# State-space mixer: C stationary in 32-column blocks, heads of a pair alternating, decay per sequence made once

## What is computed

```python
acum = jnp.cumsum(dtc * A_gr, axis=1)
decay = jnp.exp(jnp.where(causal, acum[:, :, None] - acum[:, None, :], -jnp.inf))
cb = jnp.einsum('btgn,bsgn->btsg', Cc, Bc)
wts = cb[..., None] * decay * dtc[:, None]
y = jnp.einsum('btsgr,bsgrp->btgrp', wts, xc)
y = y + jnp.einsum('btgn,bgrpn->btgrp', Cc, hs) * jnp.exp(acum)[..., None]
hs = exp(acum[:, -1]) * hs + jnp.einsum('bsgr,bsgrp,bsgn->bgrpn', to_end, xc, Bc)
```

## Time and profile before

| | us |
|---|---|
| median of 3 runs | 3431.39 |
| lowest, highest | 3429.54, 3434.74 |
| span of the profiled execution | 3425.9 |
| state-space stage in it | about 1534 to 2484 |

### The profile page before, as it was taken

The page is one execution under the profiler, slowest core; times in us unless marked ns, Lnnn a source line. Parts: engine busy times, 40 slices in busy tenths (PEclk is TensorE's granted clock), DMA queues, the critical chain, the costliest instruction groups (busy, mean ns, idle before and its releaser), DMA issues.

```text
span 3425.9 us, 64127 instructions
## 1 busy us (share of the span) xinstructions
PE 3279.2 (96%) x23449; PEld 3192.2 (93%) x23449; DVE 2114.1 (62%) x3198; ACT 1350.2 (39%) x1691; POOL 887.6 (26%) x1123
## 2 busy tenths in 40 slices
PE   7999999999999999989999999999989999999997
PEld 6999999999999999988888988988889999999997
DVE  4554556676546675567676676676666674467644
ACT  4332324444334444443343333343344543344432
POOL 2101013222102232225442343243332230023221
PEclk9999999999999999999999999998899999999999
DMA  5343435444454444544444444444434444544444
GB/s 201 137 164 135 174 114 181 147 169 162 145 173 160 171 159 147 172 166 166 157 157 158 157 163 157 168 158 170 169 119 164 166 156 151 172 168 161 161 148 145
DMA packets 91384, 545.56 MB, mean 159 GB/s; under 512 B 11688, under 2 KB 12528, under 8 KB 43904
## 3 DMA queue, kind: packets, MB, share of 16 engines
q1 hardware_dynamic: 71872, 466.98, 38.6%
q0 software_dynamic: 19392, 76.98, 6.2%
HBM read 510.92 MB, written 32.99 MB: 159 GB/s over the span
## 4 chain that ended last, share of the span: by engine, by line
PE 80%; DVE 8%; issue 6%; ACT 4%; POOL 2%; DMA 0%; DVEq 0%; POOLq 0%; ACTq 0%; SPq 0%
PE ps L388 25%; PE ps L389 24%; PE ps L390 24%; PE ps L395 7%; ACT w_hi L660 2%; DVE w_lo L983 2%; DVE b_u L1312 1%; DVE b_u L1314 1%; DVE b_u L1310 0%; DVE work L1397 0%; DVE sumsq L1392 0%; POOL sumsq L1470 0%; POOL b_xw L1614 0%; DVE b_s L1386 0%; ACT b_out_hi L937 0%
## 5 line engine op out<-in xcount | busy, mean ns | idle before, releaser
L388 PE MATMUL ps<-hn_hi,w_hi 128*128 128x288 f32 x4896 | 1481.3, 303 | 36.9 <-DVE w_lo L983 16.8
L389 PE MATMUL ps<-hn_lo,w_hi 128*128 128x288 f32 x4896 | 1461.8, 299 | 0.0
L390 PE MATMUL ps<-hn_hi,w_lo 128*128 128x288 f32 x4896 | 1456.0, 297 | 0.0
L983 DVE TENSOR_TENSOR w_lo<-w_raw,w_hi 128x2048 fp32r<-128x2048 f32 (+1 forms) x482 | 1045.0, 2168 | 593.3 <-ACT w_hi L660 593.0
L660 ACT ACTIVATE w_hi<-w_raw 128x2048 fp32r<-128x2048 f32 (+1 forms) x482 | 857.7, 1780 | 1145.2 <-PE ps L390 1140.5
L388 PEld LDWEIGHTS ps<-hn_hi,w_hi 128*128 128x128 f32 x4896 | 936.9, 191 | 45.8 <-issue 22.1
L389 PEld LDWEIGHTS ps<-hn_lo,w_hi 128*128 128x128 f32 x4896 | 938.0, 192 | 1.2
L390 PEld LDWEIGHTS ps<-hn_hi,w_lo 128*128 128x128 f32 x4896 | 938.6, 192 | 0.0
L1546 POOL COPY f_new<-f_pad 128x2 f32 x176 | 242.6, 1379 | 1080.9 <-ACT f_u L831 1080.9
L388 PE MATMUL ps<-act_hi,w_hi 128*128 128x288 f32 x1408 | 416.2, 296 | 13.8 <-DVE act_lo L1242 13.8
L389 PE MATMUL ps<-act_lo,w_hi 128*128 128x288 f32 x1408 | 418.0, 297 | 0.0
(11 more groups left out here) (261 smaller groups left out, 3462.2 us busy)
## 6 DMA issues: line engine op xcount, KB each, us to landing
w_raw<-wf_up_in SPq DMA_DIRECT2D x176, 1024.0 KB, 4.8
w_raw<-wf_down_in SPq DMA_DIRECT2D x128, 704.0 KB, 4.0
w_raw<-wb_in_in SPq DMA_DIRECT2D x80, 1024.0 KB, 4.8
w_raw<-wa_in_in SPq DMA_DIRECT2D x48, 1024.0 KB, 4.8
w_raw<-wb_out_in SPq DMA_DIRECT2D x32, 1024.0 KB, 4.8
w_raw<-wa_out_in SPq DMA_DIRECT2D x16, 1024.0 KB, 4.8
b_sT<-b_sT_in POOLq DMA_DIRECT2D x32, 512.0 KB, 4.9
b_s<-b_s_in POOLq DMA_DIRECT2D x32, 512.0 KB, 4.4
```

Of the source, the lines that this page charges most:

```text
L388: nc.tensor.matmul(out, w_hi[:, s, col], hi[:, t, :], start=first and k == 0, stop=False)
L389: nc.tensor.matmul(out, w_hi[:, s, col], lo[:, t, :], start=False, stop=False)
L390: m = nc.tensor.matmul(out, w_lo[:, s, col], hi[:, t, :], start=False, stop=end)
L983: TT(w_lo[:, s, 0:cols], w_raw[:, s, 0:cols], w_hi[:, s, 0:cols].bitcast(F32), ALU.subtract).then_inc(w_low, 1)
```

## The change

- The product of C with the carried state moves from "mix" to "sel". For each sequence b a block of 32 columns (`b_cm_of[b]`, C of its four tokens, zero elsewhere) is stationary, and the 128 columns of the sequence's state `b_sT[:, b, :]` move. Sequences share four column blocks of the array (output partitions 32g to 32g+31, g = b % 4), two accumulated on each. `b_sT_in` is awaited here. ScalarE scales the result by the decay per token and head (`b_eas`) into `b_ys`, ahead of its exponential, and one matmul with `fold` (four stacked 32x32 identities) adds it to the output's PSUM inside the mix.
- In the mix the two heads of a pair alternate block by block, and the sample block takes 128 rows of `b_xdt` and `b_dec`, whose rows past 32 are zero, for 32.
- The decay of the sample tokens and of the states is made once in `gate_columns_b`, for all heads (`b_eas`, `b_fade`), not per pair from `b_rsum` and `b_ea`; GpSimd's state decay reads `b_fade`.
- VectorE's output is one instruction where it was three.
- GpSimd adds the squares of pairs 1 and 2 to those of pair 0, and the mean takes two matmuls for four.

The load `b_sT` keeps its place in GpSimd's order. The diff, cut to the lines that change and one before them:

```diff
@@ -223,10 +224,11 @@
             b_u = sb("b_u", [P, BP], F32, st)
-            b_yi = sb("b_yi", [P, TS], F32, st)
-            b_rows = sb("b_rows", [64, 3, T], F32, st)
+            b_rows = sb("b_rows", [P, 3, T], F32, st)
             b_nac2 = sb("b_nac2", [P, T], F32R, st)
-            b_rsum = sb("b_rsum", [64, TS + 1], F32, st)
+            b_amp = sb("b_amp", [64, 1], F32, st)
+            b_fade = sb("b_fade", [P, 32, NB], F32, st)
+            b_eas = sb("b_eas", [P, 64], F32, st)
@@ -239,11 +241,14 @@
             b_xw = sb("b_xw", [P, 3, P], F32, st)
-            b_ea = sb("b_ea", [P, TS], F32, st)
         b_tmp = b_xdt[0:64, 0:2, 0:T]
+        b_ea4 = b_xdt[0:64, 0, 0:P].rearrange("p (j t) -> p j t", j=4)
+        b_spread = b_xdt[0:64, 1, 0:64 * NB]
+        b_cm = b_rows[:, 1, :].rearrange("p (b x) -> p b x", x=TS + SL)
+        b_cm_of = [b_rows[:, 1, TS * b:TS * (b + 1)] for b in range(NB)]
+        b_ys = b_rows[:, 2, 0:P]
@@ -553,14 +561,18 @@
                         m = nc.tensor.transpose(ps[0:w, M1 if n < 2 else M2, 192 * (n % 2) + 64 * b:192 * (n % 2) + 64 * b + 64],
-                                                b_rows[:, row, b * P:b * P + w], ident[0:64, 0:64])
-                m.then_inc(gb_turned, 1)
+                                                b_rows[0:64, row, b * P:b * P + w], ident[0:64, 0:64])
+                pe.wait_ge(gb_faded, 1)
+                nc.tensor.transpose(ps[:, M2, 192:256], b_xdt[0:64, 0, 0:P], ident[0:64, 0:64])
+                pe.wait_ge(gb_spread, 1)
+                mm(ps[:, M3, :], mean_mat[0:64, :], b_spread).then_inc(gb_turned, 1)
                     wait(pe, b_gvar, u)
+                    wait(pe, b_ysr, u.times(4))
@@ -581,25 +593,28 @@
                     mm(ps[:, M0, 0:T], b_sel[:, 0, :], b_nac2[:])
-                    mm(ps[:, M1, 0:T], b_sel[:, 1, :], b_nac2[:])
-                    one_head = b_sel[0:64, :, :].bitcast(F32)
-                    mm(ps[0:64, M1, T:T + TS], one_head[:, 0, 0:64], b_rsum[:, 0:TS])
-                    mm(ps[64:P, M1, T:T + TS], one_head[:, 1, 0:64], b_rsum[:, 0:TS]).then_inc(b_rowsr, 1)
+                    mm(ps[:, M1, 0:T], b_sel[:, 1, :], b_nac2[:]).then_inc(b_rowsr, 1)
+                    wait(pe, b_cmr, u.plus(1))
+                    wait(pe, b_spr, u.times(4).plus(k))
+                    wait(pe, b_sT_in, u.times(4).plus(k + 1).times(16))
+                    for b in range(NB):
+                        g = b % 4
+                        m = mm(ps[TS * g:TS * (g + 1), M3, P:2 * P], b_cm_of[b], b_sT[:, b, :], b < 4, b >= 4)
+                    m.then_inc(b_yraw, 1)
                     k = (j - 2) // 2
-                    ch = slice(k * P, (k + 1) * P)
                     wait(pe, b_yg, u.times(4).plus(k))
-                    wait(pe, b_sT_in, u.times(4).plus(k + 1).times(16))
-                    for b in range(NB):
-                        mm(ps[:, M2, T + SL * b:T + SL * (b + 1)], b_sT[:, b, :], cT[:, TP + SL * b:TP + SL * (b + 1)])
-                    for e in range(2):
-                        rows, hc = slice(64 * e, 64 * (e + 1)), slice(k * P + 64 * e, k * P + 64 * (e + 1))
+                    wait(pe, b_ysr, u.times(4).plus(k + 1))
+                    halves = [(slice(64 * e, 64 * (e + 1)), slice(k * P + 64 * e, k * P + 64 * (e + 1))) for e in range(2)]
+                    for e, (rows, hc) in enumerate(halves):
                         mm(ps[rows, M2, 0:TP], b_xdt[:, 0, hc], b_dec[:, e, 0:TP], True, False)
+                    for e, (rows, hc) in enumerate(halves):
                         mm(ps[rows, M2, P:TP], b_xdt[:, 1, hc], b_dec[:, e, TP:TP + P], False, False)
-                        m = mm(ps[rows, M2, TP:T], b_xdt[0:TS, 2, hc], b_dec[0:TS, e, TP + P:SC], False, True)
-                    m.then_inc(b_yst, 1)
+                    for e, (rows, hc) in enumerate(halves):
+                        mm(ps[rows, M2, TP:T], b_xdt[:, 2, hc], b_dec[:, e, TP + P:SC], False, False)
+                    mm(ps[:, M2, TP:T], b_ys, fold[:], False, True).then_inc(b_yst, 1)
@@ -608,11 +623,11 @@
                 if j == 9:
+                    wait(pe, b_gsum, u.plus(1).times(2))
+                    wait(pe, b_yg, u.plus(1).times(4))
+                    mm(ps[:, M2, 0:T], mean_mat[:], b_io[:, p, 2, :], True, False)
                     wait(pe, b_gsq, u.plus(1).times(4))
-                    wait(pe, b_yg, u.plus(1).times(4))
-                    for k in range(4):
-                        m = mm(ps[:, M2, 0:T], mean_mat[:], b_io[:, p, 2 + k, :], k == 0, k == 3)
-                    m.then_inc(b_gms, 1)
+                    mm(ps[:, M2, 0:T], mean_mat[:], b_io[:, p, 5, :], False, True).then_inc(b_gms, 1)
@@ -854,18 +869,19 @@
                     wait(act, proj_taken, EA_BGATE + 1)
-                    own.link(A(b_rows[:, 1, :], b_rows[:, 1, :], ACT.Identity, bias=b_small[:, 0:1]))
-                    A(b_rsum[:, TS:TS + 1], b_small[:, 1:2], ACT.Exp)
-                    own.link(A(b_tmp[:, 0, :], b_rows[:, 1, :], ACT.Abs))
-                    A(b_rows[:, 2, :], b_tmp[:, 0, :], ACT.Exp, scale=-1.0).then_inc(gb_exp, 1)
+                    own.link(A(b_rows[0:64, 1, :], b_rows[0:64, 1, :], ACT.Identity, bias=b_small[:, 0:1]))
+                    A(b_amp[:], b_small[:, 1:2], ACT.Exp)
+                    own.link(A(b_tmp[:, 0, :], b_rows[0:64, 1, :], ACT.Abs))
+                    A(b_rows[0:64, 2, :], b_tmp[:, 0, :], ACT.Exp, scale=-1.0).then_inc(gb_exp, 1)
                     act.wait_ge(gb_logs, 1)
-                    A(b_nac2[0:64, :], b_rows[:, 0, :], ACT.Copy).then_inc(gb_high, 1)
-                    A(b_rows[:, 2, :], b_rows[:, 2, :], ACT.Exp, scale=-1.0)
-                    A(b_rsum[:, 0:TS], b_rows[:, 0, TP:T], ACT.Exp, scale=-1.0).then_inc(gb_rows, 1)
+                    A(b_nac2[0:64, :], b_rows[0:64, 0, :], ACT.Copy).then_inc(gb_high, 1)
+                    A(b_rows[0:64, 2, :], b_rows[0:64, 2, :], ACT.Exp, scale=-1.0).then_inc(gb_rows, 1)
+                    A(b_ea4, b_rows[0:64, 0, TP:T].unsqueeze(1).to_broadcast([64, 4, TS]), ACT.Exp,
+                      scale=-1.0).then_inc(gb_faded, 1)
@@ -874,7 +890,12 @@
                         w = P if b < 2 else TS
-                        m = A(col[0:w, :, b, :], src[0:w, :, b, :], ACT.Copy)
+                        A(col[0:w, :, b, :], src[0:w, :, b, :], ACT.Copy)
+                A(b_eas[:], ps[:, M2, 192:256], ACT.Copy)
+                for e in range(2):
+                    rows = slice(64 * e, 64 * (e + 1))
+                    m = A(b_fade[rows, :, :], ps[rows, M3, :].rearrange("p (m e b) -> p e m b", e=2, b=NB)[:, e, :, :],
+                          ACT.Copy, scale=float(D_MODEL))
@@ -915,6 +936,14 @@
                     k = (j - 2) // 2
+                    n = u.times(4).plus(k)
+                    wait(act, b_yraw, n.plus(1))
+                    wait(act, b_yst, n.times(2))
+                    for e in range(2):
+                        head = n.times(2).plus(e).value
+                        col = slice(head, head + 1) if isinstance(head, int) else bass.ds(head, 1)
+                        m = A(b_ys[:, 64 * e:64 * (e + 1)], ps[:, M3, P + 64 * e:P + 64 * (e + 1)], ACT.Copy, scale=b_eas[:, col])
+                    m.then_inc(b_ysr, 1)
@@ -1042,6 +1071,9 @@
             TS_(b_normw[:], b_normw[:], 0.5, None, ALU.mult)
+            own.link(TT(fold[:], ident[:, 0:TS], ident[:, TS:2 * TS], ALU.add))
+            own.link(TT(fold[:], fold[:], ident[:, 2 * TS:3 * TS], ALU.add))
+            TT(fold[:], fold[:], ident[:, 3 * TS:P], ALU.add)
@@ -1258,10 +1290,11 @@
             V.memset(b_dec[:], 0.0)
+            V.memset(b_xdt[:, 2, :], 0.0)
             norm(2)
-            TT(b_rows[:, 1, :], ps[0:64, (N_BIN - 1) % 4, 0:T], rstd[0:64, :], ALU.mult).then_inc(proj_taken, 1)
-            brow = lambda n: b_rows[:, n, :] if n < 3 else b_tmp[:, n - 3, :]
+            TT(b_rows[0:64, 1, :], ps[0:64, (N_BIN - 1) % 4, 0:T], rstd[0:64, :], ALU.mult).then_inc(proj_taken, 1)
+            brow = lambda n: b_rows[0:64, n, :] if n < 3 else b_tmp[:, n - 3, :]
@@ -1279,13 +1312,16 @@
-                    own.link(TS_(brow(4), brow(1), b_rsum[:, TS:TS + 1], None, ALU.mult))
+                    own.link(TS_(brow(4), brow(1), b_amp[:], None, ALU.mult))
                     dve.wait_ge(gb_high, 1)
-                    TT(b_nac2[64:P, :], b_rows[:, 0, :], b_nac2[0:64, :].bitcast(F32), ALU.subtract).then_inc(gb_low, 1)
+                    TT(b_nac2[64:P, :], b_rows[0:64, 0, :], b_nac2[0:64, :].bitcast(F32), ALU.subtract).then_inc(gb_low, 1)
+                    dve.wait_ge(gb_faded, 1)
+                    TT(b_spread.rearrange("p (h b) -> p h b", b=NB), head_ident[0:64, :].unsqueeze(2).to_broadcast([64, 64, NB]),
+                       b_ea4[:, 0, SL - 1:TS:SL].unsqueeze(1).to_broadcast([64, 64, NB]), ALU.mult).then_inc(gb_spread, 1)
                 if j == 7:
```

(20 more changed lines are left out.)

7 lines of the change are left out of this document (4 added, 3 removed).

## The result

The changed kernel takes 3474.38 us (median of 4 runs, 3469.54 to 3486.12), the kernel before 3431.89 beside it: ratio 1.0133, 95% interval 1.0113 to 1.0152. It is slower by 42.5 us, as forecast (3472). The profiled execution has a span of 3471.7 for 3425.9.

A forecast was written before the change was run, and what follows sets the result against it. TensorE's line was taken as bound, neck and neck with VectorE's order; six steady groups 34, first group 3.5, last 0, gate columns 3.4, together 41 us on span 3425.9, plus 5.5 to the median: 3472 us, range 3425 to 3520.

The forecast's parts named there:

- The wait: Sel of pairs 1 to 3: TensorE idles 3 to 5 us for the b_sT load, some 24 times, 100 us in all.
- The steady group: Six of the eight mixed groups, walked pair by pair: each turn, 105.61 us before, grows by 5.7 us.
- The clock's p: Projection behind each b_sT wait: what the lowered clock adds, 2.2 to 3.8 us, taken as 2.5.
- the columns: New 32-column matmuls in sel: four column blocks at once, 0.75 us per pair.
- The rival of no overlap: Column blocks and heads run serially: sel 2.0 us, b_dec 1.65, 4.6 more per group, 3507 us; chance 0.12.
- The groups: State-space stage: six steady groups add 34 us, the first group 3.5, the last about 0.
- The gate columns: Once, before TensorE restarts at the gate columns: spread product, 512-column matmul, copies and three more add 3.4 us.
- The squares: Two of four mean matmuls go, 1.0 us per group; GpSimd's additions, 1.5 us each, cost nothing or lie under the exponential.
- The other side: Rival: the load is in time, each group gains 4 us, 32 in all, less 3.4, giving 3403 us; chance 0.12.

The follow-up runs named there:

- the early load: Changed kernel with GpSimd issuing the b_sT load of the next pair one step earlier, behind the b_s load: 3389.9 us, ratio 0.988 to the kernel before.
- The filled wait: Changed kernel with 24 projection-size matmuls that nobody reads ahead of TensorE's b_sT wait in pairs 1 to 3: 3457.42 us, ratio 1.0083.

## Why the prediction came out as it did

**The wait** was the prediction's core, and it stands: 24 waits for `b_sT` of 4.7 us in the mean, 113.5 in all (predicted 3 to 5 each, 100 in all), and the early load removes both them and the loss. The load lands 6.0 to 7.3 us behind the additions, 6.6 in the mean (predicted 6.2).

**The steady group**: 111.39 us for 111.3 predicted. Within it, counted from the turn's start, the column groups of pairs 1 to 3 were to be done at 47.4, 70.2 and 93.0 us; the trace has 49.1, 71.1 and 93.7. A pair takes 22.0 and 22.6 us for 22.8.

**Terms of that agreement were off, against each other**, so its 0.1 us is in part luck. The clock's p was too high: behind the three waits the projections lose 2.1, 1.4 and 2.0 us (8.54, 7.88 and 8.43 for 6.46) and the columns up to 0.4 more, some 2 for the 2.5 taken; over all 21 waits with one projection behind them it is 1.6 and the columns. The filled wait bounds it from below at 17 us in all, 0.7 per wait. Against that the first column group came 1.7 us late: pair 0's additions ended 41.3 us into the turn for 40.4, the load landed 6.76 behind them for 6.2, and the columns took 1.01 for 0.75.

**The matmuls.** The mix is 2.05 us (predicted 2.1), `b_dec` 0.89 (0.8), the columns 0.57 at full clock (0.75), and the fold costs 0.24 (0.3). The rival of no overlap falls, as the row of the early load's kernel shows best, where no wait stands ahead of the records:

```profile
L403 PE MATMUL ps<-b_sT,b_rows 128*32 128x128 f32 x512 | 22.2, 295 | 0.0
```

One record lasts 295 ns and all 512 together 22.2 us, a seventh of their sum. The rule of the Trainium skill, "TensorE: Matmul & The Clock Gate", section "What overlaps and what doesn't", that a weight load overlaps running matmuls only when its row group differs, stood for the 2.0 us of one after the other. This trace speaks against it: all these blocks use all rows, and in the group at 1665.58 the weight loads of the second four start 1665.61 to 1665.63, while the first four matmuls run (to 1665.88). Against that 2.0, an estimate, the 0.57 is 3.5 times as fast, within the up to 4x that the Trainium skill gives for 32 columns ("TensorEngine Tiling (Array Packing)", "Theoretical Speedup"). What I missed in `b_dec` is that the uniform rows carried the larger part.

**The groups.** By the starts of the groups' first mean matmuls the seven differences are +5.8, +4.5, +6.8, +3.1, +6.2, +7.3 and -0.6 us, 33 in all; I had six of 5.7 and one of 0, 34. The first group gave +4.3 for 3.5.

**The gate columns**: TensorE restarts at 1542.20 for 1533.68, 8.5 us later, but 3.7 of it came before the stage (the last projection ahead of it ends at 1531.9 for 1528.2), where the change touches nothing on TensorE's line. The stage's own part is 4.8 for 3.4 predicted: the mis-sized item is the 512-column product.

```profile
1537.13 1.02 DVE L1321 TENSOR_TENSOR b_xdt<-head_ident,b_xdt 64x512 f32<-64x512 f32 x1
...
1538.21 2.07 PE L403 MATMUL ps<-b_xdt,mean_mat 64*128 64x512 f32 x2 [5.55 <-DVE b_xdt L1321]
...
1542.20 0.61 PE L396 MATMUL ps<-hn_hi,w_hi 128*128 128x288 f32 x1 [1.92 <-ACT b_fade L897]
```

The spread product takes 1.02 (0.7 taken), and the product behind 5.55 us of idle takes 2.07 (0.9 taken), at the low clock. So the sum, 45.8 us of span for 41, is short by 1.4 here, 3.7 that no edit explains and 0.8 in the first group, less 1 in the others. The 3.7 are not the change's own work: that projection ends at 1528.2, 1529.6 and 1534.9 in the kernel before and the two built on it, and between 1529.4 and 1535.4 in the changed kernel and the nine built on it. The same program in two experiments gives 1529.6 and 1529.8, so it is hardly scatter either; what moves it stays open. Without it the change put 42.1 us onto the span, for 41 predicted.

**The squares** were put at 1.0 us per group gained, their GpSimd work at nothing, under the wait. In the changed kernel this holds (about 11 us in eight groups for 8). The reason given for it, that VectorE's slower taps lie under the later exponential, is also what limits it: with the early load the cover is gone, and the additions cost 6 to 7 us. GpSimd's addition lasts 0.8 us, not the 1.5 that I took from L1470.

**The other side**, the load in time, was priced at 3403 and the early load measured 3390. I had given 4 us per group, 32, to all savings together; the alternation and the 128 rows alone gained 21 in the kernel before, and the early load shows 39 with the additions of the squares still costing 6 to 7. I had taken VectorE's order as the bound, with 0.56 us per pair to give. That TensorE's shorter mix also lets the next split begin sooner, and so shortens VectorE's line, is my reading of the missing 13; no run takes it apart.

## What to carry to other kernels

When an edit moves a reader of a transfer ahead, the transfer's issue has to move with it: compare the time from what permits the issue to the landing with the time at which the new reader arrives, and read whether the removed work would have covered it; here 70 us less of matmuls were worth less than one load left in its place. A cover is a property of the state of the kernel: the same pre-addition on another engine gained about 11 us while TensorE stood for the load and lost about 6 once it didn't, so re-measure the side edits after the main wait is gone. The fastest version was all of the change with the load issued a step earlier and without the pre-added squares, 3381 to 3383 us, 1.3 to 1.4% under the kernel before.
